# The first mixer of a two-layer diffusion backbone: scores moved ahead of pooling and conditioning, four conditioning blocks to a PSUM bank

## The chip, the cores and the metric

One NeuronCore of a Trainium2 chip runs the whole kernel. The metric is the device time of one execution in microseconds (us), lower is better. Five queues matter: TensorE (PE in the profile), VectorE (DVE), ScalarE (ACT), SyncE (SP, which issues nearly all transfers) and the 16 DMA engines behind it. Engines run in order, each its own list, and wait for each other through semaphores.

## The reference

Two kinds of tokens pass two layers: 128 context tokens and 256 latent tokens, 384 rows of 1024 features, three row tiles of 128 in the kernel. Layer 0, cut to what the change touches:

```python
m = silu(cond) @ ada_w[l] + ada_b[l]          # 6 x 1024 per layer: shift, scale, gate, for mixer and for MoE
h = rmsnorm(x, g) * (1 + scale) + shift
q, k, v, u = split(h @ w_in)                  # 512 + 128 + 128 + 512 columns
q, k = rmsnorm(q), rmsnorm(k); rope on latent tokens
o  = sink_softmax(q k^T / 8) v                # 8 heads, 2 key heads; tile 0: 128 keys, tiles 1, 2: 384 keys
p  = ((window_mean(u) - u) @ pool_w[g]) * pool_scale   # 4 groups, windows 2, 4, 8, 16
x  = x + gate * (concat(o, p) @ w_out)
```

Then a mixture of experts (MoE), then layer 1 with a Fourier mixer and a second MoE. `silu(cond) @ ada_w` is a vector by matrix product: nearly all of its cost is 48 MB of weights, and it can be computed long before it is used.

## The kernel before

**Weights.** A ring of 7 slots of 2 MB (`ring`, `NS = 7`) takes all large weights in one order. SP issues block n (`weights`, L850) when block n - 7 has had its last use on TensorE. Blocks 7 to 20 of that order are the conditioning blocks 4 to 17 (list `ADA`), 21 and 22 are `a_w_out`, 23 to 25 conditioning blocks 18 to 20, and the experts follow.

**Conditioning.** `ada_product(n)` multiplies block n with the two condition vectors, 8 matmuls of 512 columns that use 32 columns of the array each, four side by side (L1861). The result is four partial rows in one bank. For a shift or scale block ScalarE copies the bank to `ada_row` (L1005), `ada_read(n)` transposes it in four pieces (L1886), and VectorE sums and combines it into `mcol` (L1334 to L1342). For a gate block (chunks 4, 5, 10, 11; here products 4 and 5) ScalarE takes one part (L1001), VectorE adds the other (`gate_parts`, L1353), and TensorE spreads it over the partitions with two matmuls (L1874), which ScalarE copies out (L1016).

**The first mixer.** The token product z = h w_in ends at L2347. Behind it TensorE's list runs: conditioning product 4; four pooling products with a banded matrix (L2364 for context, L2367 for latent tokens, two of 256 columns) each followed by the map with `pool_w` (L2356) of the group before; products 5 and 6 with their read-backs; the transposes of k and q (L2381 to L2386); then per row tile i and half of the heads `scores(i, half)` (L2399), with conditioning products between, and `values(i, half)`: four transposes of the probabilities (L2409) and the products with v (L2420). ScalarE copies every pooling result (L1121, L1124) and transposed tile (L1084) and runs the exponentials (`exps`, L1074, L1075). VectorE empties the scores (L1729 for tile 0, L1732 with mask for tiles 1 and 2), takes maxima (L1739 to L1744, after which semaphore `p_max` lets `exps` go) and normalizes (L1750 to L1756, then `p_ready` lets `values` go).

**Banks and order.** The order is written out by hand three times, for TensorE, ScalarE and VectorE, and once in `plan()`, which hands out PSUM banks in turn (`Turns`). Before a bank is filled again, `begin` makes TensorE wait until its last content has been emptied. The output product `project(0)` (L1922) comes behind `ada_read(17)`, then the residual, the norm, the router (`route`) and the MoE.

Of the kernel before, what the change touches and what calls it, by code (L numbers as in the profile page):

```python
# [39 lines left out]
NPG = 4  # L40
ZW = AW + 2 * KVW + PW
# [36 lines left out]
GATES = [n for n in range(len(ADA)) if ADA[n][1] in GATE_CHUNKS]  # L78

# [115 lines left out]
class Turns:  # L195
# [27 lines left out]

    def empty(self, key):
        who = self.of[key][2]
        self.emptied[who] += 1
        self.of[key][3] = self.emptied[who]
# [15 lines left out]
def plan():  # L243
# [3 lines left out]
    def ada_product(n):  # L247
        t.add(("ada", n), "dve" if n in GATES else "act")

# [107 lines left out]
    ada_product(4)  # L357
    for g in range(NPG):
        t.add(("pool", g), "act")
        if g > 0:  # L360
            t.add(("pooled", g - 1), "act")
    t.add(("pooled", NPG - 1), "act")
    ada_product(5)
    ada_read(4)
    ada_product(6)
    ada_read(5)
    ada_read(6)
    t.add("kT", "act")
    for c in range(NH // 2):
        t.add(("qT", c), "act")  # L370

# [4 lines left out]
    def values(i, half, between=None):  # L376
        for n in range(4 * half, 4 * half + 4):
            t.add(("PT", i, n), "act")
        if between:
            ada_read(between)  # L380
        if half:
            t.add(("oT", i), "dve", bank=7)

    scores(0, 0)
    scores(0, 1)
    ada_product(7)
# [22 lines left out]
    ada_read(17)  # L409
    project(0)  # L410
# [40 lines left out]
def build(nc, x_prompt, x_sample, cache_k, cache_v, ada_w,  # L451
# [37 lines left out]
    with ctx:  # L489
# [37 lines left out]
        cond = sb("cond", [P, KT, 32])  # L527
# [24 lines left out]
        pooled = PC[:, 0:6, :].rearrange("p a n -> p (a n)").rearrange("p (b n) -> p b n", b=2)  # L552
# [423 lines left out]
        def _(act):  # L976
# [16 lines left out]
            def ada_product(n):  # L993
                if n >= 2:

                    act.wait_ge(full, read_turn(n - 2)[1])
                if n in GATES:

                    bank, filled = turn[("ada", n)][0:2]
                    act.wait_ge(full, filled)  # L1000
                    act.activation(gate_row[:, n % 2, :], banks[bank][:, :], ACT.Identity, scale=con("row_sign"))\  # L1001
# [3 lines left out]
                emptied_inc(act.activation(ada_row[:, n % 2, :], b[:, :], ACT.Copy))  # L1005
# [19 lines left out]
            def affine(s, t):  # L1025
                l, f = s // 2, s % 2
                act.wait_ge(affine_ready, 4 * (s + 1))
# [87 lines left out]
            ada_product(4)  # L1115
            for g in range(NPG + 1):
                if g < NPG:
                    b = stage_bank(("pool", g), act)
                    if g >= 2:
                        act.wait_ge(full, turn[("pooled", g - 2)][1])  # L1120
                    emptied_inc(act.activation(pooled[:, g % 2, :], b[:, 0:TOK], ACT.Copy))  # L1121
                if g > 0:
                    b = stage_bank(("pooled", g - 1), act)
                    emptied_inc(act.activation(T[:, 4 + g - 1, :], b[:, 0:TOK], ACT.Identity,  # L1124
                                               scale=colv[:, R_PS + g - 1:R_PS + g]))
            ada_product(5)
            ada_read(4)
            ada_product(6)
            ada_read(5)
# [6 lines left out]
            ada_product(7)  # L1136
            exps(0, 1)
            ada_product(8)
            ada_product(9)
            turned(0, 0)  # L1140
            exps(1, 0)
            ada_product(10)
            turned(0, 1)
            exps(1, 1)
            ada(11, 13)
            turned(1, 0)
            exps(2, 0)
            ada_product(13)
            ada(14, 16)
            turned(1, 1)  # L1150
            exps(2, 1)
            ada_product(16)
            turned(2, 0)
            ada_product(17)
            turned(2, 1)
# [129 lines left out]
        def _(dve):  # L1285
# [39 lines left out]
            def ada_read(n):  # L1325
# [5 lines left out]
                src = b[:, :].rearrange("p (s q r) -> p s r q", s=4, q=4)[:, :, 0:2, :]  # L1331
                f, k0 = cc // 6, 2 * (cc % 6)
                m = mcol[:, l, f, k0:k0 + 2]
                emptied_inc(dve.tensor_reduce(m.rearrange("p k v c -> p (k v) c"), src, AX.X, ALU.add))  # L1334
# [3 lines left out]
                dve.tensor_tensor(m, m, bias[:, k0:k0 + 2, :].unsqueeze(3).to_broadcast([P, 2, 2, 2]), ALU.add)  # L1338
                settle()
                at = (R_MIX, R_FFN)[f] + l * KT + k0  # L1340
                gain = colv[:, at:at + 2].unsqueeze(2).to_broadcast([P, 2, 2])
# [7 lines left out]
            def gate_parts(n):  # L1349
                dve.wait_ge(gate_high, GATES.index(n) + 1)  # L1350
                b = stage_bank(("ada", n), dve)
                row = gate_row[:, n % 2, :]
# [300 lines left out]
            for k, r in enumerate((R_CCTX, R_C)):  # L1653
                twice = cond[:, :, 0:4].rearrange("p k (d c) -> p k d c", d=2)[:, :, :, k]
# [63 lines left out]
            gate_parts(4)  # L1718
            gate_parts(5)
            ada(4, 7)  # L1720
# [51 lines left out]
            ada_read(9)  # L1772
            scores(1, 1)
            normalize(1, 0)
            ada_read(10)
            attended(0)
            scores(2, 0)
            ada(11, 13)
            normalize(1, 1)
            scores(2, 1)  # L1780
            ada_read(13)
            ada(14, 16)
# [3 lines left out]
            ada_read(16)  # L1786
            attended(2)
            ada_read(17)
# [40 lines left out]
        def _(pe):  # L1829
# [16 lines left out]
            def ada_product(n):  # L1846
# [6 lines left out]
                b = begin(("ada", n))  # L1853
# [18 lines left out]
            def gate_read(n, k):  # L1872
                b = begin(("gate", n, k))
                pe.matmul(b[:, :], spread[:, k, :], gate_row[:, n % 2, :], start=True, stop=True).then_inc(full, 1)  # L1874

            def ada_read(n):
                done_by(("ada", n))
                row = ada_row[:, n % 2, :]
# [479 lines left out]
            ada_product(4)  # L2358
            pe.wait_ge(special_in, 16)
            done_by(("z", 2, 2))  # L2360
            for g in range(NPG):
# [7 lines left out]
                if g > 0:  # L2369
                    pooled_map(g - 1)  # L2370
            pooled_map(NPG - 1)
            ada_product(5)
            ada_read(4)
            ada_product(6)
            ada_read(5)
            ada_read(6)
# [11 lines left out]
            done_by("kT")  # L2388
# [12 lines left out]
            def values(i, half, between=None):  # L2401
# [25 lines left out]
                if between:  # L2427
                    ada_read(between)
# [4 lines left out]

            scores(0, 0)
            scores(0, 1)
            ada_product(7)
            ada_product(8)
            ada_read(7)
            scores(1, 0)
            ada_read(8)  # L2440
            ada_product(9)
            values(0, 0, 9)
            scores(1, 1)
            ada_product(10)
            values(0, 1, 10)
# [131 lines left out]
```

## Time and profile before

| | us |
|---|---|
| median of 3 runs | 786.59 (786.29 to 787.45) |
| profiled execution: span, first to last instruction | 785.1 |
| token product z ends, first mixer's stretch begins | 79.38 |
| output product `project(0)` begins | 147.94 |

The profile shows one execution. It gives no total time of that execution beside the span; the median of the runs is 1.5 us above the span. "Idle before" in a row is the time in which the engine stood still before the instruction, with the one that released it. The granted clock is 1.00 where TensorE has 2.4 GHz and 0.50 where it has 1.2 GHz.

### The profile page before, as it was taken

Reading aid. Unit: us, or ns where it says so; the run is one execution under the profiler, and the core shown is the slowest. Engines: PE = TensorE matmul, PEld = TensorE weight load, DVE = VectorE, ACT = ScalarE, POOL = GpSimd, SP = SyncE. Lnnn points to the kernel's source line nnn. Section 1 sums busy time; section 2 is a strip of 40 time slices with the busy share of each in tenths; the row PEclk is TensorE's granted clock in tenths of the full one; section 3 lists DMA queues with packets and bytes.
Section 4 is the critical chain, followed back from the end, with each engine's and each line's share of the span. In section 5 each row is a group of like instructions: output and inputs, shape, how many; then the busy total and the mean of one; then the engine's idle time right before and its main releaser. Section 6 shows DMA issues by size and latency. Waiting matters only on the chain.

```text
span 785.1 us, 10152 instructions
## 1 busy us (share of the span) xinstructions
PE 764.6 (97%) x3991; PEld 377.2 (48%) x3991; DVE 343.4 (44%) x783; ACT 177.8 (23%) x440; POOL 2.2 (0%) x9
## 2 busy tenths in 40 slices
PE   7999999999999999999999999999999999999997
PEld 3364535545553444444345657645544444345334
DVE  2216188214841742643345412326732643445326
ACT  4111566205521111101112601105221101111111
POOL 0000000000000000000000000000000000000000
PEclk9999999999999999999999999999999999999999
DMA  8979999942899999999999982024599999999994
GB/s 347 427 220 429 430 426 426 427 169 100 330 368 407 425 429 429 427 425 428 425 415 425 425 351 107 1 108 192 203 387 422 427 424 428 428 426 426 425 415 189
DMA packets 32851, 277.12 MB, mean 353 GB/s; under 512 B 7789, under 2 KB 8833, under 8 KB 12833
## 3 DMA queue, kind: packets, MB, share of 16 engines
q1 hardware_dynamic: 32305, 275.02, 85.0%
q10 hardware_dynamic: 432, 1.28, 0.4%
q8 instruction: 34, 0.56, 0.3%
q0 software_dynamic: 64, 0.13, 0.0%
q14 instruction: 16, 0.13, 0.0%
HBM read 274.72 MB, written 1.70 MB: 352 GB/s over the span
## 4 chain that ended last, share of the span: by engine, by line
PE 85%; DMA 5%; DVE 4%; ACT 2%; issue 1%; SPq 1%; DVEq 1%; ACTq 0%
PE bank L2052 27%; PE bank L2077 13%; PE bank L1922 11%; PE bank L2031 5%; PE bank L2083 5%; PE bank L2484 5%; PE bank L2347 4%; PE bank L1861 4%; DMA ring<-in_moe_w 3%; DMA ring<-in_ada_w 3%; PE bank L2308 2%; PE bank L2399 1%; PE bank L2063 1%; PE bank L2420 1%; PE bank L2058 1%
## 5 line engine op out<-in xcount | busy, mean ns | idle before, releaser
L2052 PE MATMUL bank<-ring,Z 128*64 128x512 f32 x1024 | 226.5, 594 | 0.6 <-DMA ring<-in_moe_w 0.6
L2052 PEld LDWEIGHTS bank<-ring,Z 128*64 128x64 f32 x1024 | 72.2, 137 | 137.8 <-issue 135.7
L2077 PE MATMUL bank<-ring,Z 128*64 128x512 f32 (+1 forms) x544 | 114.0, 571 | 0.0
L1922 PE MATMUL bank<-ring,T 128*128 128x512 f32 x192 | 83.1, 592 | 0.0
L2077 PEld LDWEIGHTS bank<-ring,Z 128*64 128x64 f32 x544 | 37.5, 137 | 68.4 <-issue 66.5
L1534 DVE TENSOR_TENSOR Z<-Z,bank 128x512 f32<-128x512 f32 x16 | 11.0, 687 | 120.0 <-PE bank L2052 120.0
L1922 PEld LDWEIGHTS bank<-ring,T 128*128 128x128 f32 x192 | 36.2, 190 | 44.0 <-issue 44.0
L2083 PE MATMUL bank<-ys,Cs 128*128 128x512 f32 (+1 forms) x204 | 52.3, 391 | 1.1 <-DVE ys L1551 1.1
L1564 DVE TENSOR_TENSOR x<-x,bank 128x512 f32<-128x512 f32 x84 | 52.1, 680 | 0.3
L1176 ACT ACTIVATE ys<-wg 128x512 fp32r<-128x512 f32 (+1 forms) x34 | 20.6, 606 | 131.2 <-DVE wg L1546 131.2
L1528 DVE COPY Z<-bank 128x512 f32<-128x512 f32 x24 | 16.6, 692 | 73.8 <-PE bank L2031 73.8
L1861 PE MATMUL bank<-ring,cond 128*32 128x512 f32 x384 | 45.8, 598 | 2.4 <-DMA ring<-in_ada_w 2.1
L2031 PE MATMUL bank<-Sel,h_high 128*128 128x256 f32 x168 | 43.7, 297 | 0.0
L1172 ACT ACTIVATE Z<-bank 128x512 f32<-128x512 f32 x16 | 9.6, 598 | 144.3 <-PE bank L2058 144.3
L2031 PE MATMUL bank<-Sel,h_low 128*128 128x256 f32 x168 | 41.0, 281 | 0.0
L2083 PEld LDWEIGHTS bank<-ys,Cs 128*128 128x128 f32 x204 | 34.7, 188 | 11.5 <-issue 4.4
L2031 PEld LDWEIGHTS bank<-Sel,h_high 128*128 128x128 f32 x168 | 31.6, 188 | 11.4 <-issue 11.4
L2484 PE MATMUL bank<-T,ring 128*128 128x384 f32 x112 | 36.3, 486 | 0.0
L1546 DVE TENSOR_TENSOR wg<-bank,wg 128x512 f32<-128x512 f32 (+1 forms) x34 | 22.4, 660 | 28.4 <-PE bank L2077 28.0
L1372 DVE TENSOR_TENSOR special<-bank,gate_b 128x512 f32<-128x512 f32 x12 | 8.3, 691 | 55.3 <-PE bank L1922 55.3
L2031 PEld LDWEIGHTS bank<-Sel,h_low 128*128 128x128 f32 x168 | 31.7, 189 | 0.0
L2347 PE MATMUL bank<-ring,T 128*128 128x256 f32 (+1 forms) x96 | 31.1, 486 | 0.0
(249 smaller groups left out, 752.5 us busy)
## 6 DMA issues: line engine op xcount, KB each, us to landing
ring<-in_moe_w SPq DMA_DIRECT2D x62, 2048.0 KB, 15.8
ring<-in_moe_w SPq DMA_DIRECT2D x60, 1024.0 KB, 11.8
ring<-in_ada_w SPq DMA_DIRECT2D x23, 2048.0 KB, 17.9
ring<-in_moe_w SPq DMA_DIRECT2D x16, 512.0 KB, 20.3
ring<-in_a_w_out SPq DMA_DIRECT2D x2, 2048.0 KB, 16.7
ring<-in_f_w_in SPq DMA_DIRECT2D x2, 2048.0 KB, 27.8
ring<-in_f_w_out SPq DMA_DIRECT2D x2, 2048.0 KB, 30.9
ring<-in_ada_w SPq DMA_DIRECT2D x2, 1024.0 KB, 8.2
```

Source lines behind the costliest of these rows:

```text
L1176: act.activation(ys[0:w, 0, a:e], wg[0:w, a:e], ACT.Copy).then_inc(s["down_high"], 1)
L1528: dve.tensor_copy(xT[:, q % 2, 2 * step:2 * step + 2, :], psX[step % 2][:, :].rearrange("p (k s) -> p k s", k=2)).then_inc(s["x_cols"], 1)
L1546: dve.tensor_tensor(wg[0:w, a:e], end_banks[n][0:w, 0:e - a], wg[0:w, a:e], ALU.mult)\
L1564: dve.tensor_tensor(a, a, out[n][:, :], ALU.add).then_inc(s["back_out"], 1)
L1861: last = pe.matmul(b[32 * q:32 * q + 32, :], cond[:, k, :], w[:, k, :], start=(k < 4), stop=(k >= 4 and not gate), skip_group_check=True)
L1922: last = pe.matmul(b[:, :], T[:, k, i * P:(i + 1) * P], w[:, k, :], start=(k == 0), stop=(k == KT - 1))
L2031: last = pe.matmul(out[:, (k - k0) * w:(k - k0 + 1) * w], rows_, Sel[:, t, 0:w], start=(t == 0 and part == 0), stop=(t == NT - 1 and part ...
L2052: last = pe.matmul(out[BLK * u:BLK * (u + 1), :], xT[:, b, k, s0 + BLK * u:s0 + BLK * (u + 1)], w[:, k, :], start=(k == 0), stop=(k == KT ...
L2077: last = pe.matmul(out, aT[:, k, BLK * u:BLK * (u + 1)], down_columns(w2, k, a, e), start=(k == 0), stop=(k == FC - 1), skip_group_check=True)
L2083: last = pe.matmul(bank[:, 0:e - a], Cs[0:w, b, t * P:(t + 1) * P], ys[0:w, part, a:e], start=(part == 0), stop=(part == 1))
L2347: last = pe.matmul(b[:, 0:wd], T[:, k, i * P:(i + 1) * P], w[:, k, :], start=(k == 0), stop=(k == KT - 1))
L2484: last = pe.matmul(b[:, 0:TOK], w[:, k, q * P:(q + 1) * P], T[:, k, :], start=(k == 0), stop=(k == KT - 1))
```

## The change

1. The transposes of k and q come right behind the token product, then two pooling products and one map, then the scores of tile 0. The other two pooling products, three maps and conditioning products 4 to 17 are spread behind and between the scores and values of the three tiles. The lists of ScalarE and VectorE follow.
2. Conditioning blocks 6 to 9, 10 to 13 and 14 to 17 (all shift and scale) each share bank 6: the condition vectors stand in a wider zero-padded tile, so that block n of four lands in other rows of the same 32, and the four products accumulate in one bank. There is one copy and one read-back for four blocks. The weights are laid out so that the four form one regular pattern. The other banks in turn are 0 to 5.
3. Each latent pooling product covers only the 136 columns that its 128 rows reach, instead of 256.
4. The pooled values stand in `T[:, 0:2]` instead of the probabilities' tile.

```diff
+POOL_REACH = [(0, SEQ + 8), (SEQ - 8, 2 * SEQ)]
+JOINED_BANK = 6
+JOINED = [range(n, n + 4) for n in (6, 10, 14)]
+FIRST_OF = {n: g[0] for g in JOINED for n in g}
+LAST_OF = {n: g[-1] for g in JOINED for n in g}
+COND_AT = 12
...
 (TensorE)
+                first, ending = FIRST_OF.get(n, n), LAST_OF.get(n, n)
+                b = begin(("ada", ending)) if n == first else banks[JOINED_BANK]
+                at = COND_AT - 4 * (n - first)
...
-                    last = pe.matmul(b[32 * q:32 * q + 32, :], cond[:, k, :], w[:, k, :],
-                                     start=(k < 4), stop=(k >= 4 and not gate), skip_group_check=True)
+                    last = pe.matmul(b[32 * q:32 * q + 32, :], cond[:, k, at:at + 32], w[:, k, :],
+                                     start=(k < 4 and n == first), stop=(k >= 4 and n == ending and not gate),
+                                     skip_group_check=True)
...
-                for q in range(2):
-                    last = pe.matmul(b[:, SEQ:TOK], z[:, 1 + q, cs], bl[:, g, q, :], start=(q == 0), stop=(q == 1))
+                for q, (a, e) in enumerate(POOL_REACH):
+                    last = pe.matmul(b[:, SEQ + a:SEQ + e], z[:, 1 + q, cs], bl[:, g, q, a:e],
+                                     start=(q == 0), stop=(q == 1), skip_group_check=True)
...
+            pool(0)
+            pool(1)
+            pooled_map(0)
+            done_by("kT")
             scores(0, 0)
             scores(0, 1)
+            pool(2)
+            pooled_map(1)
+            pool(3)
+            pooled_map(2)
+            pooled_map(3)
+            ada_product(4)
+            scores(1, 0)
+            ada_product(5)
+            ada_read(4)
+            values(0, 0)
+            scores(1, 1)
+            ada_product(6)
+            ada_read(5)
+            values(0, 1)
             ada_product(7)
+            scores(2, 0)
             ada_product(8)
-            ada_read(7)
-            scores(1, 0)
-            ada_read(8)
+            values(1, 0)
             ada_product(9)
-            values(0, 0, 9)
-            scores(1, 1)
+            scores(2, 1)
+            ada_read(9)
             ada_product(10)
-            values(0, 1, 10)
-            scores(2, 0)
-            ada(11, 13)
-            values(1, 0)
+            values(1, 1)
+            ada_product(11)
+            ada_product(12)
+            values(2, 0)
             ada_product(13)
-            scores(2, 1)
+            values(2, 1)
+            ada_product(14)
             ada_read(13)
-            ada(14, 16)
-            values(1, 1)
+            ada_product(15)
             ada_product(16)
-            values(2, 0)
-            ada_read(16)
             ada_product(17)
-            values(2, 1)
             ada_read(17)
             project(0, N_WOUT)
...
 (ScalarE, behind the copies of kT and qT)
+            pool(0)
+            pool(1)
+            pool_map(0)
             exps(0, 0)
+            pool(2)
+            pool_map(1)
             exps(0, 1)
+            pool(3)
+            pool_map(2)
+            pool_map(3)
+            ada_product(4)
+            ada_product(5)
+            ada_read(4)
             turned(0, 0)
             exps(1, 0)
+            ada_read(5)
             turned(0, 1)
             exps(1, 1)
...
 (VectorE)
             scores(0, 0)
             scores(0, 1)
-            ada_read(7)
             normalize(0, 0)
+            gate_parts(4)
             dve.wait_ge(kv_out_done, 32)
             scores(1, 0)
-            ada_read(8)
+            gate_parts(5)
             normalize(0, 1)
```

## Rows read from the trace of the kernel before

**Rows 1.** Windows: stretch, length, busy (instructions) PE, PEld, DVE, ACT, POOL, clock, DMA, GB/s.

```profile
79.38:147.94 68.56, 65.89 (x557) 35.49 (x558) 38.21 (x123) 39.64 (x111) 0.00 (x0) 1.00 1.01 427
160.00:170.00 10.00, 10.00 (x24) 4.37 (x23) 2.72 (x4) 0.00 (x0) 0.00 (x0) 1.00 0.15 41
```

**Rows 2.** Chain of waits, 79 to 148 us: start, us, what.

```profile
79.38 1.85 PE bank L1861 x16
81.23 0.22 PE bank L1867 x8
...
90.86 0.66 PE bank L1874 x2
...
93.82 0.61 ACT ada_row L1005
...
101.94 0.59 PE bank L1886 x4
102.53 1.50 PE bank L2399 x8
...
142.00 1.90 PE bank L1861 x16
```

**Rows 3.** Groups, TensorE, 79.38 to 148: instruction, count | busy, mean ns | idle before, releasers.

```profile
L1886 PE MATMUL bank<-cst,ada_row 128*128 128x128 f32 x48 | 7.8, 285 | 1.5 <-ACT ada_row L1005 1.2 <-issue 0.3
...
L2399 PE MATMUL bank<-Z 64*128 64x384 f32 x32 | 6.2, 508 | 0.7 <-DVE mcol L1334 0.6
```

**Rows 4.** Timeline of TensorE: start, us, instruction, [idle before, releaser].

```profile
82.58 0.38 PE L2364 MATMUL bank<-special,Z 128*128 128x128 f32 x2
82.80 1.03 PE L2367 MATMUL bank<-special,Z 128*128 128x256 f32 x4
83.66 0.81 PE L2356 MATMUL bank<-PC,pool_ws 128*128 128x384 f32 x2
...
94.97 0.49 PE L2381 MATMUL bank<-cst,h 128*128 128x128 f32 x3
...
96.81 1.56 PE L2399 MATMUL bank<-Z 64*128 64x128 f32 x16
```

**Rows 5.** Timeline of ScalarE, the same columns.

```profile
82.78 0.49 ACT L1121 ACTIVATE PC<-bank 128x384 f32<-128x384 f32 x1 [0.51 <-PE bank L2367]
...
97.75 1.28 ACT L1074 ACT_TABLE_LOAD   x1
99.57 0.40 ACT L1074 ACTIVATE PC<-PC,small 128x128 f32<-128x128 f32 x1 [0.54 <-DVE small L1744]
...
101.13 0.19 ACT L1075 ACTIVATE small<-small 128x4 f32<-128x4 f32 x1
```

**Rows 6.** Timeline of VectorE, the same columns.

```profile
73.08 0.82 DVE L1715 TENSOR_TENSOR h<-h,Z 128x640 f32<-128x640 f32 x1
82.30 0.75 DVE L1353 SCALAR_TENSOR_TENSOR gate_row<-bank,cst,gate_row 128x512 fp32r<-128x512 f32 x1 [8.40 <-ACT gate_row L1001]
...
97.33 0.88 DVE L1729 TENSOR_SCALAR PC<-bank 128x128 f32<-128x128 f32 x4 [1.47 <-PE bank L2399]
...
104.63 1.95 DVE L1732 SCALAR_TENSOR_TENSOR h<-bank,special 128x384 f32<-128x384 f32 x4
...
108.88 0.18 DVE L1334 TENSOR_REDUCE mcol<-bank 128x8 f32<-128x32 f32 x1
```

**Rows 7.** SP's issue of block 20 of the ring (conditioning block 17) and its time to landing.

```profile
L850 SPq DMA_DIRECT2D ring<-in_ada_w x1: 328/328/328, 112.6 to 112.6; - x1
...
DMA to landing us min/median/max: 15.7/15.7/15.7
```

**Rows 8.** Windows at the end of the span, the columns of rows 1.

```profile
781.00:782.00 1.00, 0.00 (x0) 0.00 (x0) 0.89 (x3) 0.00 (x0) 0.00 (x0) 1.00 0.14 51
782.00:783.00 1.00, 0.00 (x0) 0.00 (x0) 0.00 (x0) 0.00 (x0) 0.00 (x0) 0.88 0.91 340
```

**Rows 9.** The same view near the start of the span.

```profile
9.00:16.00 7.00, 4.93 (x29) 1.85 (x29) 1.67 (x8) 2.33 (x5) 0.00 (x0) 1.00 1.03 425
```

More of the change, by code:

```diff
@@ L247, in ada_product @@
     def ada_product(n):
-        t.add(("ada", n), "dve" if n in GATES else "act")
+        if n not in LAST_OF:
+            t.add(("ada", n), "dve" if n in GATES else "act")
+            return
+        last = LAST_OF[n]
+        if n == FIRST_OF[n]:
+            t.fill(("ada", last), "act", bank=JOINED_BANK, whole=False)
+        if n < last:
+            t.part(("ada", n), ("ada", last))
+        else:
+            t.whole(("ada", last))
+            t.empty(("ada", last))
     def ada_read(n):
@@ L356, in plan, with scores, values, pool @@
             t.add(("z", c, i), "act" if i % 2 or c == 2 else "dve")
[L357 to L367, printed above, removed]
+    def scores(i, half):
+        for n in range(4 * half, 4 * half + 4):
+            t.add(("score", i, n), "dve")
+    def values(i, half):
+        for n in range(4 * half, 4 * half + 4):
+            t.add(("PT", i, n), "act")
+        if half:
+            t.add(("oT", i), "dve", bank=7)
+    def pool(*groups):
+        for g in groups:
+            t.add(("pool", g), "act")
+    def pooled(g):
+        t.add(("pooled", g), "act")
+    t.banks = list(range(JOINED_BANK))
     t.add("kT", "act")
@@ L370, in plan @@
         t.add(("qT", c), "act")
-    def scores(i, half):
-        for n in range(4 * half, 4 * half + 4):
-            t.add(("score", i, n), "dve")
[L376 to L382, printed above, removed]
+    pool(0, 1)
+    pooled(0)
     scores(0, 0)
     scores(0, 1)
+    pool(2)
+    pooled(1)
+    pool(3)
+    pooled(2)
+    pooled(3)
+    ada_product(4)
[7 more added lines that the diff above has]
+    values(0, 1)
     ada_product(7)
+    scores(2, 0)
     ada_product(8)
-    ada_read(7)
-    scores(1, 0)
-    ada_read(8)
+    values(1, 0)
     ada_product(9)
-    values(0, 0, 9)
-    scores(1, 1)
+    scores(2, 1)
+    ada_read(9)
     ada_product(10)
-    values(0, 1, 10)
-    scores(2, 0)
-    ada(11, 13)
-    values(1, 0)
+    values(1, 1)
+    ada_product(11)
+    ada_product(12)
+    values(2, 0)
     ada_product(13)
-    scores(2, 1)
+    values(2, 1)
+    ada_product(14)
     ada_read(13)
-    ada(14, 16)
-    values(1, 1)
+    ada_product(15)
     ada_product(16)
-    values(2, 0)
-    ada_read(16)
     ada_product(17)
-    values(2, 1)
     ada_read(17)
+    t.banks = list(range(7))
     project(0)
@@ L1000, in ada_product @@
                     act.wait_ge(full, filled)
-                    act.activation(gate_row[:, n % 2, :], banks[bank][:, :], ACT.Identity, scale=con("row_sign"))\
+                    act.activation(gate_row[:, ROW_OF[n], :], banks[bank][:, :], ACT.Identity, scale=con("row_sign"))\
                        .then_inc(gate_high, 1)
@@ L1114, in _, with pool, pool_map @@
                 z_copy(2, i)
[L1115 to L1129, printed above, removed]
+            def pool(g):
+                b = stage_bank(("pool", g), act)
+                if g >= 2:
+                    act.wait_ge(full, turn[("pooled", g - 2)][1])
+                emptied_inc(act.activation(pooled[:, g % 2, :], b[:, 0:TOK], ACT.Copy))
+            def pool_map(g):
+                b = stage_bank(("pooled", g), act)
+                emptied_inc(act.activation(T[:, 4 + g, :], b[:, 0:TOK], ACT.Identity, scale=colv[:, R_PS + g:R_PS + g + 1]))
             b = stage_bank("kT", act)
@@ L1873, in gate_read @@
                 b = begin(("gate", n, k))
-                pe.matmul(b[:, :], spread[:, k, :], gate_row[:, n % 2, :], start=True, stop=True).then_inc(full, 1)
+                pe.matmul(b[:, :], spread[:, k, :], gate_row[:, ROW_OF[n], :], start=True, stop=True).then_inc(full, 1)
             def ada_read(n):
                 done_by(("ada", n))
-                row = ada_row[:, n % 2, :]
+                row = ada_row[:, ROW_OF[n], :]
                 if ADA[n][1] in GATE_CHUNKS:
@@ L2356, in pooled_map, with pool @@
                 pe.matmul(b[:, 0:TOK], pool_ws[:, g, :], pooled[:, g % 2, :], start=True, stop=True).then_inc(full, 1)
[L2358 to L2361, printed above, removed]
+            def pool(g):
                 b = begin(("pool", g))
@@ L2387, in _ @@
                 last.then_inc(full, 1)
-            done_by("kT")
+            pe.wait_ge(special_in, 16)
+            done_by(("z", 2, 2))
             def scores(i, half):
@@ L2399, in scores, with values @@
                     pe.matmul(b[:, 0:keys.shape[1]], q, keys, start=True, stop=True).then_inc(full, 1)
-            def values(i, half, between=None):
+            def values(i, half):
                 pe.wait_ge(p_ready, 2 * i + half + 1)
```

117 lines of the change are left out of this document (59 added, 58 removed).

## The prediction

> **What bounds the kernel now.** I read the windows first. From the end of the token product at 79.38 us to the output product at 147.94 us TensorE is busy for 65.89 of 68.56 us, at the full clock, while VectorE and ScalarE work 38 and 40 us and the DMA engines never rest [rows 1]. Then the chain of waits: it runs through TensorE's own instructions, with short pieces of another engine between, typically the 0.61 us copy of a conditioning row ahead of its read-back [rows 2]. So this stretch is TensorE's list plus 2.67 us in which it stands. The timelines give the price of each instruction and show who waits. Last the transfers: the share of 1.01 in the stretch could mean that weights set its end, so I looked at when blocks land. Block 20 (conditioning block 17) is issued at 112.6 and lands 15.7 later, at 128.3 [rows 7]; its product starts at 142.0 [rows 2]. At 160 to 170 the DMA share is 0.15, the ring is full [rows 1]. Weights lead by 14 us at the end of the stretch. TensorE's list bounds it.
>
> **What is removed.** Twelve read-backs of four transposes become three. One is 0.59 us [rows 2], so nine save 5.3 us. Eight latent pooling matmuls go from 256 to 136 columns: a pair costs 0.86 us, start to start (82.80 to 83.66; the row's 1.03 overlaps the next by 0.17), the context product before it 0.22 [rows 4]. By columns a pair saves 0.86 x 120/256 = 0.40, four pairs 1.6 us. Bounds of the second: nothing, if a narrower matmul is no cheaper, and 1.6; I take 1.6, since 128 and 256 columns stand at 0.22 and 0.43 in these rows. Sum of work removed: 6.9 us. Conditioning products, scores, values and maps are the same instructions in another order. A product that accumulates into a shared bank streams the same 512 columns: no price, and I bound it by 0.1 us a product either way, 1.2 in all.
>
> The waits ahead of read-backs that go with them (an `ada_row` copy only just done, or the score bank that waited for a sum on VectorE) make 1.8 of the 2.67 us idle: 1.2 and 0.6 [rows 3]; 0.9 stays.
>
> Nine copies of 0.61 on ScalarE [rows 2] and nine sums of three small operations on VectorE go as well; both engines have slack in the old order except where the softmax chain runs, so this gives room and no time of its own. The joined sum takes 128 values instead of 32: at most 0.3 us more, bounded by the 0.22 of a 128-column eviction (0.88 for four [rows 6]), three times, each behind other work.
>
> **What is added: waits.** I walk the new order with the durations above, 0.12 us from TensorE's end to another engine's start and 0.06 back (the same walk of the old order ends within 1.2 us of the trace, so only its difference is used).
>
> The transposes of k and q take 1.84 (94.97 to 96.81) [rows 4] and need VectorE's last rotation, done at 73.9 [rows 6]: no wait where pooling covered it before. Two pooling products at 0.68 and a map at 0.65 (0.81 less the overlap [rows 4]) bring TensorE to 83.2, the scores of tile 0 (1.5) to 84.7, and pool 2, map 1 and pool 3 to 86.7.
>
> *Map 2* needs ScalarE's copy of pool 2, and that now stands behind `exps(0,0)`. VectorE starts on the scores at 83.5, and from there to the first exponential are 2.2 (97.33 [rows 6] to 99.57 [rows 5]), so 85.7. Four exponentials and the small one take 1.65 (99.57 to 101.13 and 0.1) [rows 5]: 87.35. The copy takes 0.49 [rows 5]: 87.85. The table load of 1.28 [rows 5] lies ahead, from 83.8 to 85.1, and is covered by the maxima; uncovered it would cost up to 1.3. TensorE waits 1.2. *Map 3* needs the copy of pool 3, behind `exps(0,1)`: the map copy to 88.25, exponentials to 89.9, copy to 90.4. TensorE was free at 88.55: it waits 1.9. Map 3 ends at 91.1.
>
> *The bank of the fourth transpose.* Product 4 with its bias takes 2.1 [rows 2] to 93.2, `scores(1,0)` 1.5 to 94.7, product 5 2.1 to 96.8, the two spreading matmuls 0.66 [rows 2] and three transposes 0.45 to 97.9. The fourth transposed head of `values(0,0)` takes the bank of product 5. That is emptied by `gate_parts(5)`, which stands on VectorE behind `scores(1,0)`, which stands behind `gate_parts(4)`, which waits for product 4 and ScalarE's part. So: ScalarE 94.0, VectorE 94.75 (0.75 [rows 6]), masked scores and maxima 4.25 (104.63 to 108.88 [rows 6]) to 99.0, `gate_parts(5)` to 99.75. TensorE waits 1.85, and 0.2 more for the copy behind it. Queued behind the wait are `scores(1,1)`, for which VectorE stands ready at 101.0, so it loses 0.3 us only.
>
> *Smaller ones.* In `values(0,1)` the copies of the transposed heads stand behind two 512-column copies of the gate (0.5 each back to back): 0.85 wait. The last read-back waits 0.8 for its copy (0.49 to 0.61 plus two handovers), where the copy was done in time before; nothing else is left to do there.
>
> Sum of added waits: 1.2 + 1.9 + 1.85 + 0.2 + 0.85 + 0.8 = 6.8; with the 0.3 us that stood at the old last read-back counted once, 6.5. Later the walk has no wait over 0.15: from tile 1 on TensorE is the late one, VectorE waits for `scores(2,0)` and `scores(2,1)`, and the probabilities of each half are ready 3 to 5 us ahead of `values`.
>
> **Transfers.** Product 4 ends at 93.2 instead of 81.5, so block 14 is issued 11.7 later and the DMA engines run dry for a few us. Each block is 2.1 MB, 4.9 us at 427 GB/s [rows 1]. Block 20 is issued behind product 10, at about 121, and lands by 131; product 17 starts at 141. The output weights land by 140, the second half is needed at 165. The hole costs nothing as long as the lead of 10 us stands, and the ring is full again by about 165, where it stood idle before [rows 1]. So the gain passes on whole: SP's later issues all follow TensorE's last use of a slot.
>
> **Sum.** 6.9 + 1.8 - 6.5 = 2.2 us. The output product starts at 145.7, the span becomes 782.9, and with the 1.5 us between the span of before and the median of its runs, the median 786.6 becomes 784.4.
>
> **Rivals.**
>
> A, *the waits are not there*. If ScalarE got the copies of pools 2 and 3 done ahead of the exponentials and banks came free in time, 6.9 + 1.8 = 8.7 less the 0.8 of the last read-back leaves 7.9: 778.7. Against: the written order puts the copies behind. If half of the 5.7 us that lie between is gained, 781.5.
>
> B, *no change*. The removed work is cheaper than priced. Sixteen transposes back to back take 1.84 [rows 4], 0.11 each, so a read-back within other transposes is worth 0.44: 1.35 less; and if the 136 columns gain nothing, 0.8 less (half of the 1.6 only moves into the waits for ScalarE). 2.2 - 2.15 = 0.05: 786.5. For: TensorE is a pipeline and rows overlap. Against: 0.59 from start to start [rows 2], and columns scale.
>
> C, *the clock falls*. Between 86.7 and 90.45 TensorE does 0.65 us of work and stands 3.1. No stretch of the old kernel is as empty while work goes on. The thinnest is the start, where 9 to 16 us has 4.93 of 7 us busy, and the clock stays 1.00 [rows 9]. From 781 on TensorE does nothing; the granted clock is still 1.00 from 781 to 782, and 0.88 in the next us, so it fell to 0.50 about 782.8 [rows 8]. If it goes to 1.2 GHz at the wait for map 3, what follows takes twice as long: product 4 alone +2.1, which VectorE's chain passes on: 786.5. If it lasts to the end of product 5, TensorE loses 2.1 + 1.5 + 2.1 = 5.7; the wait of 1.85 at the bank falls away but VectorE's chain is 2.1 later too, so the end moves by 4.6: 789.0, slower than before. It decides from where the lower level outlasts `scores(1,0)`. No row shows how long it would last.
> The Trainium skill, TensorE: Matmul & The Clock Gate, section "HAM oscillation", says that idle gaps of some length put the array back to half rate and that the next work then starts cold. The rows of the end agree that it falls with idleness; whether two waits with one map between them are enough no row shows. By that rule the time is that of C, by the busy start it is the forecast.
>
> D, *weights late*: a lead of 10 us would have to vanish. That takes transfers at under 350 GB/s. 3 in 100.
>
> **How the numbers follow.** Forecast 784.4: 0.45. A: 0.08. B: 0.19. C: 0.24, half of it near no change, half slower. D and what I have not seen: 0.04, slower. What can be told from no change is about 0.2%, 1.6 us, so faster is below 785.0. Faster 0.45 + 0.08 = 0.53, less a little of the forecast that falls short: 0.51. Same 0.19 + 0.12 = 0.31 with that little. Slower 0.18. The likeliest case's own range is 783.2 to 785.3. The range to hold 8 in 10 goes from the half-way case of A, 781.9, to 788.2 within C.
>
> **What would show it.** In the changed kernel's trace: L1886's transposes in the stretch 12 instead of 48; latent pooling pairs near 0.46; idle ahead of the maps of groups 2 and 3 (1.2 and 1.9), released by ScalarE's copies; idle ahead of the fourth transpose of tile 0 (1.85), released by VectorE's gate row; the output product at 145.7; DMA share below 1 from about 93 on. A granted clock under 1.00 between 88 and 98 would be C. The prediction is wrong if the stretch's end moves by less than 1.6, if a probability wait appears ahead of `values` in tiles 1 and 2, or if what is gained at 146 is not there at the end.

## The result, and the profile after

The changed kernel takes 788.5 us (median of 12 runs, 787.55 to 792.14) where the kernel before takes 786.7. The ratio of the two is 1.0034, 95% interval 1.0022 to 1.0046: it stands above that of the medians, 1.0023, because five of the 12 runs are longer than the rest, and it leaves out one slow run of the kernel before, at 2768.89 us. The kernel is slower by 0.2 to 0.3%; the forecast was 784.4, with a range of 781.9 to 788.2. In the profiled execution the span is 786.2 us, against 785.1 before.

The first mixer did nearly what was forecast. Windows of the kernel after (columns of [rows 1]; the token product ends 0.3 us earlier in this execution than in that of the kernel before, so the stretch begins at 79.08):

```profile
79.08:145.90 66.82, 60.04 (x522) 30.63 (x520) 33.77 (x96) 33.99 (x102) 0.00 (x0) 1.00 0.94 389
160.00:170.00 10.00, 10.00 (x25) 4.46 (x24) 2.44 (x4) 0.00 (x0) 0.00 (x0) 1.00 0.80 311
```

TensorE is busy for 60.04 us instead of 65.89 and idle for 6.8 instead of 2.7. The stretch is 1.7 us shorter (66.82 against 68.56). The granted clock is 1.00 all through. TensorE's timeline in the kernel after (columns of [rows 4]) has each wait of the walk at its place:

```profile
80.90 0.63 PE L2408 MATMUL bank<-special,Z 128*128 128x136 f32 x4
81.36 0.38 PE L2405 MATMUL bank<-special,Z 128*128 128x128 f32 x2
...
87.96 0.91 PE L2400 MATMUL bank<-T,pool_ws 128*128 128x384 f32 x2 [0.99 <-ACT T L1158]
90.43 0.91 PE L2400 MATMUL bank<-T,pool_ws 128*128 128x384 f32 x2 [1.56 <-ACT T L1158]
...
99.99 0.33 PE L2444 MATMUL bank<-cst,PC 128*128 128x128 f32 x1 [2.02 <-DVE gate_row L1401]
...
106.41 0.78 PE L2455 MATMUL bank<-Z 128*64 128x128 f32 x8 [0.85 <-ACT Z L1123]
...
145.25 0.66 PE L1930 MATMUL bank<-cst,ada_row 128*128 128x128 f32 x4 [0.78 <-ACT ada_row L1044]
145.74 4.46 PE L1966 MATMUL bank<-ring,T 128*128 128x512 f32 x10
```

The group of the read-backs, which answers to the first of [rows 3], and the scores' have

```profile
L2434 PE MATMUL bank<-Z 64*128 64x384 f32 x32 | 6.2, 508 | 0.0
...
L1930 PE MATMUL bank<-cst,ada_row 128*128 128x128 f32 x12 | 2.0, 287 | 0.8 <-ACT ada_row L1044 0.8
```

The output product starts 2.0 us earlier than before (the timelines' starts are 145.74 and 147.77); 0.3 of these are the earlier end of the token product, which is no work of the change. Of that lead 1.75 is left at the first gather of the experts (206.07 and 207.82), 1.48 at the second (554.70 and 556.18), and 1.41 at the last products ahead of the last pair of experts of the second layer (743.36 and 744.77). What the change itself loses on this way are two waits for VectorE, one at the router of each layer. The kernel before:

```profile
194.16 1.09 PE L1903 MATMUL bank<-cst,h 128*128 128x128 f32 x8 [0.17 <-DVE h L1301]
553.18 0.19 PE L1971 MATMUL bank<-Ms,before_bf 128*128 128x64 bf16 x1 [0.39 <-DVE Ms L1465]
```

and after:

```profile
192.40 1.09 PE L1947 MATMUL bank<-cst,h 128*128 128x128 f32 x8 [0.44 <-DVE h L1341]
551.70 0.19 PE L2015 MATMUL bank<-Ms,before_bf 128*128 128x64 bf16 x1 [0.70 <-DVE Ms L1513]
```

Each of the two executions also waits once for weights, 0.45 us at 384.08 after and 0.56 at 410.65 before. Experiment 4's trace has no such wait later than 60 us and experiment 5's one of 0.3, so these belong to the execution more than to the kernel.

Then the lead is lost at one place. TensorE before, the last products ahead of the last pair of experts of the second layer, and the first products of that pair:

```profile
744.77 7.09 PE L2077 MATMUL bank<-ring,Z 128*64 128x512 f32 x32
751.69 7.04 PE L2052 MATMUL bank<-ring,Z 128*64 128x512 f32 x32
```

and after:

```profile
743.36 7.09 PE L2121 MATMUL bank<-ring,Z 128*64 128x512 f32 x32
752.89 7.09 PE L2096 MATMUL bank<-ring,Z 128*64 128x512 f32 x32 [2.45 <-issue]
```

A lead of 1.41 us has become a lag of 1.20. "issue" is idle time for which the profile has no releaser. Between the two pairs TensorE's program loads the number of overflow blocks and, since it is zero, jumps over their code, 275 instruction slots. The profile's queues show code being fetched there. There is one packet of code in each of two windows, kernel before in 747.2 to 747.3 us and kernel after in 750.2 to 750.3 (queue and kind: packets, MB, share of the DMA engines):

```profile
q8 instruction: 1, 0.02, 68.7%
```

```profile
q8 instruction: 1, 0.02, 68.8%
```

Before, the fetch comes 4.6 us ahead of the end of the row (751.86), with work still queued. After, it comes 0.2 us ahead of the end of the row at 750.45, where the array has run dry, and the array works again 2.6 us after the fetch.

**Code pieces.** A packet is 16 KB. Over TensorE's compiled program I count one slot for an instruction, two for a matmul with its weight load and four for one in f32: 8703 slots after, 90 fewer than before (8793). The page of the profile has 34 packets and 0.56 MB of code, so 64 bytes a slot and 256 slots a packet. The jump of the second layer stands at slot 8207 before and 8117 after: 15 and 181 past a multiple of 256. I write "remainder 15" and "remainder 181". The count starts at the program's first instruction; at which remainder of it a fetched piece begins, it doesn't tell.

### The profile page after: what moved, and what is told of

Read it like the earlier page. It is cut to its first block, busy times and chain, and to the rows that moved or that the text cites. A ratio compares the mean times of both kernels' runs of the same rounds, so it can differ in the third digit from the quotient of the medians.

```text
span 786.2 us, 9990 instructions
## 1 busy us (share of the span) xinstructions
PE 761.3 (97%) x3955; PEld 374.5 (48%) x3955; DVE 339.0 (43%) x756; ACT 172.3 (22%) x431; POOL 2.3 (0%) x9
## 4 chain that ended last, share of the span: by engine, by line
PE 85%; DMA 5%; DVE 4%; ACT 2%; issue 1%; DVEq 1%; SPq 1%; ACTq 0%
PE bank L2096 27%; PE bank L2121 13%; PE bank L1966 10%; PE bank L2075 5%; PE bank L2127 5%; PE bank L2531 5%; PE bank L2391 4%; PE bank L1904 4%; DMA ring<-in_ada_w 3%; DMA ring<-in_moe_w 2%; PE bank L2352 2%; PE bank L2455 1%; PE bank L2434 1%; PE bank L2107 1%; PE bank L2102 1%
```

## The experiments

In the first three, and in 10 and 11, only the length of TensorE's program differs. Waits on a semaphore long reached are spread through the first token product, where they cost nothing that shows:

```
 for k in range(KT):
+    for _ in range(n):                 # the program is 84, 252, 168, 42 or 126 slots longer
+        pe.wait_ge(cond_rows, 1)
     last = pe.matmul(b[:, 0:wd], T[:, k, ...], w[:, k, :], ...)
```

**1. The change, 84 slots longer (remainder 9).**

> The changed kernel with 84 waits on a long-reached semaphore spread through TensorE's first token product (TensorE's program becomes 84 instructions longer, the work is the same). Theory (code): the 2.45 us for which TensorE stands before the last pair of the second layer's experts is the fetch of the code that the skipped overflow block's jump lands in, and it depends on where that jump falls in 256-instruction pieces of the program; at 84 more the jump is at remainder 9 of 256, where the kernel before has it at 15, so the stand goes to under 0.3 us, the lead of 1.4 us at 743 us reaches the end, and the time is 785.0 to 785.6. Rival (timing): the stand comes of the shifted stream of weights, whatever the code's place: 2.4 us again and 788.5. Rival (chance): the time is 788.5 +- 1 and the stand appears in some executions of either.

Median 786.99, ratio to before 1.0000 (0.9988 to 1.0012). The stand is gone (no idle over 0.5 us ahead of the last pair). But the 12 runs fall apart: those with a mean granted clock of 0.999 take 784.93 to 785.68, as expected; four at 0.996 to 0.998 take 786.98 to 787.54; three at 0.992 to 0.993 take 789.5 to 789.6. The profiled one is of the last kind. Its windows (columns of [rows 1]):

```profile
88.00:90.00 2.00, 0.80 (x2) 0.18 (x2) 1.00 (x5) 2.00 (x11) 0.00 (x0) 0.94 0.99 418
90.00:92.00 2.00, 1.65 (x6) 0.57 (x10) 0.00 (x0) 0.77 (x2) 0.00 (x0) 0.50 0.25 107
92.00:96.00 4.00, 4.00 (x27) 0.99 (x26) 0.00 (x0) 0.58 (x1) 0.00 (x0) 0.50 0.00 0
```

The mean clocks put the fall to 1.2 GHz towards the end of the wait for map 3; it is back at 2.4 GHz between 96 and 98 us (0.85 in that window), and this execution reaches the output product at 149.91 instead of 145.74. The same waits (0.99 and 1.56) with the clock at 1.00 all through are in the trace of the changed kernel. So the fall comes in some executions. The stand before the last pair is not its reason, since here there is none. Below, "undisturbed" runs are those whose mean granted clock is 0.999 or 1.000. The kernel after has it too: seven runs at 0.999 or 1.000 take 787.55 to 788.58, five at 0.993 to 0.996 take 789.38 to 792.14. No trace of these five exists, so that their clock falls at the same place is likely and not shown.

The Trainium skill, TensorE: Matmul & The Clock Gate, section "HAM oscillation", has a matmul kernel whose array falls back to half rate in its waits for data and starts the next tile cold. This trace agrees in kind (0.50 behind 0.99 + 1.56 us of idle), with other work in the way and not each time.

**2. The change, 252 slots longer (remainder 177).**

> The changed kernel with 252 such waits, one code piece of 256 instructions but for 4: the jump falls at remainder 177 where the changed kernel has 181. Theory (code): the stand of 2.4 us stays and the time is 788.0 to 789.0. Rival (timing): also 788.5. Rival (the waits themselves act, not the place): as with 84 waits or further off, 785 or less than 788.

789.23 (ratio 1.0034, 1.0021 to 1.0048), just above the 788.0 to 789.0 that was expected, and 787.51 to 788.32 for the four runs at a clock of 1.000; the other six have 0.993 to 0.998. The stand is back, 2.07 us after one matmul of the last pair. More waits than in experiment 1, and the loss returns: the waits themselves don't act, the place to which they move the jump does.

**3. The kernel before, 168 slots longer (remainder 183).**

> The kernel before with 168 such waits: its jump falls at remainder 183 of 256, beside the changed kernel's 181. Theory (code): it now takes the stand before the last pair of the second layer's experts, 2 to 2.7 us, and the time rises from 786.7 to about 788.5 to 789.5. Rival (timing): 786.7, no stand.

789.03 (six runs, 788.91 to 789.75), ratio 1.0031 (1.0019 to 1.0042). The kernel before, with none of the change, is given the loss:

```profile
743.99 7.09 PE L2078 MATMUL bank<-ring,Z 128*64 128x512 f32 x32
753.70 7.09 PE L2053 MATMUL bank<-ring,Z 128*64 128x512 f32 x32 [2.62 <-issue]
```

**4. The kernel before with the narrowed pooling alone.**

```
-for q in range(2):
-    last = pe.matmul(b[:, SEQ:TOK], z[:, 1 + q, cs], bl[:, g, q, :], ...)
+for q, (a, e) in enumerate(((0, SEQ + 8), (SEQ - 8, 2 * SEQ))):
+    last = pe.matmul(b[:, SEQ + a:SEQ + e], z[:, 1 + q, cs], bl[:, g, q, a:e], ...)
```

> The kernel before with only the narrowed pooling products (136 columns a matmul instead of 256; the order, the banks and the length of TensorE's program stay). By the prediction's term this removes 1.6 us from TensorE's pooling stretch: output product at 146.3 and 785.1 if it passes on whole; if the wait on ScalarE's copies of pooled maps takes it back, 786.7. The code theory says only that no new stand appears, since the program's length is unchanged: 785.1 to 786.7.

785.08, ratio 0.9979 (0.9971 to 0.9988). The output product starts at 146.32, 1.45 earlier, and all of it reaches the end (1.5 us between the medians). A latent pair now takes 0.47 from start to start, against 0.86:

```profile
81.64 0.63 PE L2367 MATMUL bank<-special,Z 128*128 128x136 f32 x4
82.11 0.39 PE L2364 MATMUL bank<-special,Z 128*128 128x128 f32 x2
```

**5. The change without TensorE's jump in the second layer.**

```
-blocks = pe.value_load(...)
-with pe.If(blocks > 0):
+if l == 0:
+    blocks = pe.value_load(...)
+    with pe.If(blocks > 0):
```

> The changed kernel with TensorE's block for overflow experts of the second layer left out (none overflows here, so it never runs): TensorE has no value load and no taken jump before the last pair there, and the program before that point is the same instruction for instruction. Theory (code): the stand of 2.45 us before the last pair is the jump's; without it at most 0.3 us, and runs without a clock fall come at 785.0 to 785.6, as with 84 waits more. Rival: the stand is a matter of where the stream of weights or the pair's own waits are; it stays and the time is 787.8 to 788.5.

Median 786.05, ratio 1.0001 (0.9990 to 1.0013); the six undisturbed runs take 784.93 to 785.86. Every instruction up to the jump stands at the slot at which the changed kernel has it, and TensorE goes from one row to the next without idle:

```profile
743.53 7.09 PE L2121 MATMUL bank<-ring,Z 128*64 128x512 f32 x32
750.44 7.04 PE L2096 MATMUL bank<-ring,Z 128*64 128x512 f32 x32
```

**6. The change with its waits mended (remainder 9).** TensorE's order, with ScalarE's and VectorE's to match:

```
-... map 0, scores(0,0), scores(0,1), pool 2, map 1, pool 3, map 2, map 3,
-product 4, scores(1,0), product 5, read 4, values(0,0), ..., read 5, values(0,1)
+... map 0, pool 2, map 1, scores(0,0), pool 3, map 2, scores(0,1), product 4, map 3,
+product 5, scores(1,0), read 4, values(0,0), ..., values(0,1), read 5
-product 14, read 13, product 15, product 16, product 17, read 17
+product 14, product 15, product 16, product 17, read 13, read 17
```

> The changed kernel, 84 slots longer, with four places of the first mixer's order changed: ScalarE copies pools 2 and 3 and scales maps 1 and 2 ahead of the first exponentials, TensorE has product 4 between maps 2 and 3 and scores (0,0) and (0,1) between the pools; gate product 5 comes ahead of scores (1,0) on both engines, so that the fourth transposed head finds its bank empty; the second half of tile 0's values goes ahead of gate 5's read; row 13 is read back beside row 17. Walked from the durations of the trace, TensorE's idle before the output product falls from 6.9 to 2.7 us: output product at 141.5 to 142, 4.2 us earlier than in the changed kernel. Theory (clock falls by the waits of 1.0 and 1.6 us at 87 to 90): no run with a fallen clock, all between 780.5 and 782. Rival (the clock falls whatever the order): some runs 2 to 4 us longer. Rival (weights late once TensorE is faster): output product at 142 but under 2 us of it left at the end, 784.

781.12 (six runs, 780.21 to 782.89), ratio 0.9933 (0.9921 to 0.9946). The output product starts at 141.23, after 1.8 us of idle in the stretch (61.85 us, 60.04 busy), slightly better than expected. The maps no longer wait:

```profile
86.84 0.71 PE L2440 MATMUL bank<-Z 64*128 64x128 f32 x8
87.49 1.92 PE L1905 MATMUL bank<-ring,cond 128*32 128x512 f32 x16
89.23 0.40 PE L1912 MATMUL bank<-brows,cst 96*32 96x128 f32 x8
89.56 0.91 PE L2406 MATMUL bank<-T,pool_ws 128*128 128x384 f32 x2
```

One run of the six, at 782.89, has a clock of 0.994, so the expectation that none would have it failed; where it fell there isn't known, since no trace of that run exists.

**7. The old order with both cuts (remainder 9).** Product 4, pooling, products 5 and 6, then the scores, as in the kernel before; joined bank and narrow pooling as in the change.

> The order of the kernel before (product 4, pooling, products 5 and 6, then scores) with both cuts of the change, the four blocks in one bank (9 read-backs gone) and the narrowed pooling products, 84 slots longer as in the first experiment. Terms of the prediction: 5.3 and 1.6 us off TensorE, none of the order's added waits; the hand walk gives the output product 7.4 us earlier than in the kernel before, at 140.5. Theory (the order cost what the cuts gave): 786.6 - 7.4 = 779.2, range 778.5 to 780.5, and no fallen clock. Rival (read-backs were cheap, the waits of the change were its own slack): output product at 144 or later and 783 or more. Rival (weights late): 140.5 but 782 or more at the end.

780.06 (779.34 to 780.46), ratio 0.9916 (0.9903 to 0.9929): the fastest of all, and no run under a clock of 0.998. TensorE in its first mixer and at its last two pairs:

```profile
79.38:140.50 61.12, 59.69 (x521) 30.71 (x522) 33.91 (x96) 35.07 (x102) 0.00 (x0) 1.00 1.01 427
```

```profile
737.48 7.09 PE L2123 MATMUL bank<-ring,Z 128*64 128x512 f32 x32
744.39 1.89 PE L2098 MATMUL bank<-ring,Z 128*64 128x512 f32 x8
```

TensorE is nearly as busy as in the kernel after (59.69 against 60.04) and stands for 1.4 us instead of 6.8. The output product starts at 140.36, and the lead of 7.4 over the trace of the kernel before is still 7.3 at 737.48. Between the medians only 6.4 of it shows (786.45 and 780.06): the trace of the kernel before has the 0.56 us wait for weights that others lack, and the second router waits 0.69 here too.

**8. The change, with pools ahead of the exponentials on ScalarE alone (remainder 9).**

```
 pool_map(0)
-exps(0, 0); pool(2); pool_map(1); exps(0, 1); pool(3); pool_map(2); pool_map(3)
+pool(2); pool_map(1); pool(3); pool_map(2); pool_map(3); exps(0, 0); exps(0, 1)
```

> The changed kernel, 84 slots longer, with one edit on ScalarE alone: the copies of pools 2 and 3 and the scaling of maps 1 to 3 come ahead of both exponentials. TensorE's order is the change's. The waits before maps 2 and 3 (0.99 and 1.56 us) go. Theory (the waits of this change stand in for one another): the hand walk gives 2.9 us instead of 1.9 before the fourth transposed head and 1.8 us of new short waits, so the output product starts within 0.2 us of the changed kernel's, 145.7 to 145.9, and undisturbed runs come at 785.3 as in the first experiment. Rival (waits add up): output product at 143.3, 782.8. On the clock: if it is the two waits together at 87 to 91 us that let it fall, no run here has under 0.998; if any idle of this stretch does, some runs are 1.5 to 4 us longer, as in the first experiment.

787.77 (ratio 1.0014, 1.0005 to 1.0023), and all 11 runs have a clock of 0.994 or 0.995. TensorE:

```profile
95.99 0.87 PE L1919 MATMUL bank<-gate_row,spread 128*128 128x512 f32 x2 [1.17 <-DVE gate_row L1402]
96.92 1.17 PE L2450 MATMUL bank<-cst,PC 128*128 128x128 f32 x3
100.82 0.47 PE L2450 MATMUL bank<-cst,PC 128*128 128x128 f32 x1 [2.74 <-DVE gate_row L1402]
```

```profile
98.00:100.00 2.00, 0.09 (x1) 0.00 (x0) 1.85 (x4) 0.28 (x1) 0.00 (x0) 0.64 1.03 442
100.00:102.00 2.00, 1.18 (x9) 0.77 (x9) 1.85 (x9) 0.67 (x2) 0.00 (x0) 0.50 0.97 418
```

The two waits for maps are gone and product 4 starts at 89.11 instead of 91.28. But ScalarE's part of gate 4 now stands behind both exponentials (at 94.39), VectorE's chain starts later, and the fourth transpose comes at 100.82 instead of 99.99. In this execution the token product ends late, so that the first pooling product starts 0.7 us behind that of the kernel after (81.40 against 80.67); with that taken off, the fourth transpose comes at the same time within 0.1 us. What the maps gave is gone by then, which supports the first theory. That transpose waits for VectorE and not for TensorE's own work, so the clock has no part in it.

The output product's start, expected at 145.8, is 148.43. Of the 2.7 us over the 145.74 of the kernel after, 0.7 is the late start and 1.8 arises from the fourth transpose to the next conditioning product (100.82 to 105.15 against 99.99 to 102.55), at the lower clock. The expectation on the clock was too simple: it also falls without the two waits for maps. All 11 runs have the lower mean clock; in the one with a trace it falls within the wait of 2.74 us that follows one of 1.17. Behind 0.99 and 1.56 it falls in some executions only.

**9. The old order without the added slots (remainder 181).**

> The old order with both cuts, without the 84 added slots: jump at remainder 181 again. Theory (code): the stand before the last pair of the second layer is back, 2.2 to 2.7 us, and the time is 780.1 + 2.5 = 782.6, range 782.0 to 783.0. Rival (the stand belongs to the change's order and its timing): no stand, 780.1.

783.52 (782.08 to 783.85), ratio 0.9965 (0.9952 to 0.9978), above the expected 782.0 to 783.0. Same order, same bank, and the stand is back:

```profile
737.57 7.09 PE L2122 MATMUL bank<-ring,Z 128*64 128x512 f32 x32
746.94 7.09 PE L2097 MATMUL bank<-ring,Z 128*64 128x512 f32 x32 [2.29 <-issue]
```

Four of the five runs have a clock of 0.996 to 0.998 and take up to 1.8 us more than the one at 0.999, which lies in the expected range. Where their clock fell no trace shows.

**10. The change, 42 slots longer (remainder 223; in the first layer 188).**

> The changed kernel with 42 waits more: jump at remainder 223 of 256 and its target 275 slots on, at 242. Theory (code): whether the stand is there depends on this alone; between 183 (stand) and 236 (none, first layer of the kernel before) no run has shown it. I expect the stand, 2.0 to 2.7 us, because the code piece that the target is in is the same as at 181. Rival (timing): the stand also at every value.

790.22, one run. The expectation for the second layer was wrong: no stand there. But the jump of the first layer, which never stood before, is now at remainder 188, where the second layer's stands:

```profile
394.65 7.09 PE L2122 MATMUL bank<-ring,Z 128*64 128x512 f32 x32
404.50 7.92 PE L2097 MATMUL bank<-ring,Z 128*64 128x512 f32 x28 [2.76 <-issue]
```

```profile
404.50:407.00 2.50, 2.50 (x6) 0.85 (x8) 0.00 (x0) 0.00 (x0) 0.00 (x0) 0.51 1.00 405
```

The stand moved to another layer with the remainder. Behind it the clock is at 1.2 GHz for some 3 us, so the stand can cost more than itself. In the traces with the stand in the second layer the clock stays at 1.00 behind it.

**11. The change, 126 slots longer (remainder 51).**

> The changed kernel with 126 waits more: jump at remainder 51 of 256, target at 70. Theory (code): at 9 and 15 there was none; I expect none here either (under 0.3 us), since the piece of the jump was entered 51 instructions, some 5 us, ahead of it.

785.32, one run, no stand:

```profile
743.32 7.09 PE L2122 MATMUL bank<-ring,Z 128*64 128x512 f32 x32
750.24 7.04 PE L2097 MATMUL bank<-ring,Z 128*64 128x512 f32 x32
```

**All together.** Over both layers of the 13 kernels, a jump at remainder 177, 181, 183 or 188 has the stand each time, 2.07 to 2.76 us, and one at 9 to 51, 142 to 148 or 223 to 236 never. In the five profiled executions that have it, the fetch comes within 0.5 us of the array's running dry, and TensorE resumes 2.5 to 2.7 us after the fetch (750.3 to 752.89 in the kernel after, 401.9 to 404.50 in experiment 10). In experiment 7 it comes at 740.4, 4.0 us ahead of the next row, and nothing waits. A fetch at the jump is not enough by itself: in the first layer of the kernel after, at remainder 146, a packet comes at 401.7, just behind the jump, and TensorE goes on:

```profile
394.50 7.09 PE L2121 MATMUL bank<-ring,Z 128*64 128x512 f32 x32
401.42 7.04 PE L2096 MATMUL bank<-ring,Z 128*64 128x512 f32 x32
```

The Trainium skill, Runtime: NRT & Kernel Launch, section "Instruction fetch mechanics", says that code is refilled in blocks of 256 instructions and that a taken branch whose target isn't in the two-page window has to wait for a fetch. All runs here fit that rule, if the place at which a piece begins is left open. A jump over 275 slots lands in the next piece, except from the last 19 slots of a piece, from where it lands two pieces on. If pieces begin at a remainder from 189 to 196 of my count, the four places that stand, 177 to 188, are among these 19 and no other place is. The packets of code agree: laid against the compiled program, which executes as many matmuls as the trace has (3955), 13 of the 14 packets between 208 and 378 us and between 575 and 727 us of the kernel after find the array at remainders of 170 to 206, and the other at 223. So pieces change somewhere about there; the exact remainder is inferred from the stands and not measured by itself.

## Why the prediction was wrong

**Too high: work removed, 6.9.** Without the new order, both cuts take 6.2 us of TensorE's busy time (65.89 to 59.69, experiment 7). Narrow pooling was 1.6 on paper and is 1.45 alone (experiment 4). That leaves 4.7 for nine read-backs, 0.53 each instead of 0.59, between the forecast and the 0.44 of rival B. The output product moves by 7.4 in experiment 7 because 1.2 us of the old waits go too (idle 1.4 instead of 2.7). The accumulating products, bounded by 0.1 us each, cost nothing: 224 matmuls at a mean of 597 ns, as in the kernel before. In the new order the busy time is 0.35 us higher again (60.04).

**Right: the added waits, one by one.** 1.2, 1.9, 1.85, 0.85 and 0.8 were forecast; 0.99, 1.56, 2.02, 0.85 and 0.78 were measured, each with the releaser named. So rival A is out. Idle time in the stretch grew by 4.1 us, where the sum says 4.7 (6.5 - 1.8).

**Near, with some luck: the end of the stretch.** Work removed was overrated by 1.05 us and idle by 0.6, in opposite directions. The stretch shrinks by 1.7 instead of 2.2. That the output product was put at 145.7 and starts at 145.74 says less than it seems: the forecast was worked out from 147.94, and on that scale (the chain of waits) the start is 145.90; and 0.3 of it is the earlier end of the token product in this execution.

**Right: transfers.** The share falls where told, and the lead holds. Rival D is out: in experiment 7 TensorE runs 7.4 us ahead and its trace has no wait for weights but one of 0.2 us at 28.

**Wrong: "So the gain passes on whole".** It was argued from transfers of weights alone, and two things stand against it.

The small one is on the way: the waits for VectorE at the two routers are 0.44 and 0.70 us instead of 0.17 and 0.39, together 0.6. The 1.7 us of the stretch less these are 1.1; the undisturbed runs of experiments 1 and 5, which lack the stand, are 1.2 and 0.9 us faster than the median of the kernel before.

The large one is the stand. What was not looked at is that TensorE's own code is a transfer too, that the change makes its program 90 slots shorter, and that this moves a jump 600 us further on from remainder 15 to 181. That costs 2.45 us. Experiments 1 and 5 take the stand away and leave the rest: medians of the undisturbed runs 785.3 and 785.6 against 788.0, so 2.5 to 2.7 us for the stand. Experiment 3 gives the stand to the kernel before, for 2.5 us.

The sum from the forecast to the measured time: 784.4, and 0.1 for the newer median of the kernel before, 0.5 for the stretch, 0.6 at the routers, 2.45 for the stand and 0.5 for the clock (below) give 788.5. The prediction had named this as a sign of being wrong: what is gained at 146 is not there at the end.

**Half right: rival C.** It named the place (the wait for map 3) and a price of up to 4.6. The one trace in which the clock fell there, experiment 1's, has the output product 4.2 us later. In the kernel after, five of 12 runs have a lower clock and take up to 4.1 us more than the undisturbed median. They add 0.5 to the median (788.5 against 788.0). The prediction asked whether the clock falls, as if one answer held for all executions. The range ended at 788.2, so without either the stand or these five runs the median would have been inside it.

**Overlooked in the plan.** The walk was near in its differences, and it could have been used on the order that wasn't changed. It would have said that both cuts in the old order shorten the stretch by far more than the change does: 7.4 us against 1.7. The new order's waits cost 5.4 of the difference.

Still open: at which slot exactly a piece of code begins; and what in one execution decides about the clock at waits of 1.0 and 1.6 us.

## What to carry to other kernels

When an edit changes how many instructions an engine has, look at every taken jump behind it: a stand "<-issue" right after a skipped block, with a code fetch at about the time at which the array ran dry, is its mark. A few dozen waits on a semaphore long reached, ahead of the jump, move it away; here they cost nothing that could be measured. Price a cut and a reorder apart, and walk the cut in the old order first. Waits placed close together on TensorE can cost more than their sum, by the clock; look at the clock of every run, not of the profiled one alone.

## What I had not expected of the hardware

The place of one jump, modulo 256 slots of TensorE's program, is worth 2.5 us of 786 (789.03 against 786.57 for the kernel before, at 168 slots more). The same two waits leave the clock at 1.00 in one execution and take it to 0.50 in the next. And 84 extra slots of semaphore waits between matmuls show no cost: the median of experiment 1's undisturbed runs is 0.2 us below that of experiment 5's, which has none.
